# Gated recurrence: the first chunk, which holds the meta tokens, makes only its state

## What is computed

```python
h = concatenate([lead (112 zeros + 16 meta tokens), x])         # 1152 positions, nine chunks
log_f = where(valid, log(max(sigmoid(f_logit), TINY)), 0)       # decay
k     = where(valid, sigmoid(-f_logit), 0)                      # keys
# per chunk, with S the state carried in:
#   o_t = sum over s <= t of (q_t . decay(s..t) k_s) v_s  +  (q_t decay(start..t)) . S
#   S   = S * decay(whole chunk) + sum over s of decay(s..end) k_s v_s
o = rmsnorm(o, out_norm) * g
return h[:, CHUNK:]                                             # the first 128 positions are dropped
```

## Time and profile before

| | |
|---|---|
| median of the three runs shown | 3839.08 us (3838.89 to 3839.68) |
| the profiled execution's own time | 3837.87 us |
| its span, first to last instruction | 3836.2 us |
| mean granted TensorE clock | 0.976 of full speed |
| PE / PEld busy | 3654.7 us (95%) / 2955.8 us (77%) |
| DVE / ACT / POOL busy | 1888.6 us (49%) / 1240.2 us (32%) / 134.7 us (4%) |
| the stage `hg` in the span | about 2793 to 2913 us |

### The profile page before, as it was taken

The page is one execution under the profiler, slowest core; times in us unless marked ns, Lnnn a source line. Parts: engine busy times, 40 slices in busy tenths (PEclk is TensorE's granted clock), DMA queues, the critical chain, the costliest instruction groups (busy, mean ns, idle before and its releaser), DMA issues. The chain is left out here.

```text
span 3836.2 us, 49234 instructions
## 1 busy us (share of the span) xinstructions
PE 3654.7 (95%) x18404; PEld 2955.8 (77%) x18404; DVE 1888.6 (49%) x3690; ACT 1240.2 (32%) x2414; POOL 134.7 (4%) x143
## 2 busy tenths in 40 slices
PE   8999999989999999999999899998958999999999
PEld 6888888867777777777777787677947777787887
DVE  4244244363334455455555534544675657644343
ACT  3243133232323333332223434443322433233222
POOL 0000010000000000000000200000010000000000
PEclk9999999999999999999999999999978999999999
DMA  4222142221111121211111320111222322232223
GB/s 144 100 85 68 58 133 65 88 91 58 57 53 54 56 63 53 64 47 46 51 45 52 130 80 31 48 45 67 72 101 81 103 78 87 77 112 94 98 95 121
DMA packets 134598, 292.44 MB, mean 76 GB/s; under 512 B 31232, under 2 KB 70192, under 8 KB 134304
## 3 DMA queue, kind: packets, MB, share of 16 engines
q1 hardware_dynamic: 117552, 248.29, 19.4%
q0 software_dynamic: 14768, 33.49, 2.9%
q10 hardware_dynamic: 2112, 8.39, 0.6%
HBM read 244.49 MB, written 51.85 MB: 77 GB/s over the span
## 5 line engine op out<-in xcount | busy, mean ns | idle before, releaser
L142 DVE TENSOR_TENSOR all_w_lo<-all_w_raw,all_w_hi 128x1024 fp32r<-128x1024 f32 x311 | 380.6, 1224 | 289.5 <-ACT all_w_hi L137 288.8
L137 ACT ACTIVATE all_w_hi<-all_w_raw 128x1024 fp32r<-128x1024 f32 x311 | 326.7, 1051 | 504.9 <-PE om_z L152 261.5
L1076 PE MATMUL da_z<-all_hi,all_w_hi 128*128 128x512 f32 x736 | 305.9, 416 | 4.1 <-DVE all_w_lo L142 4.1
L1076 PE MATMUL da_z<-all_hi,all_w_lo 128*128 128x512 f32 x736 | 291.3, 396 | 0.0
L1076 PE MATMUL da_z<-all_lo,all_w_hi 128*128 128x512 f32 x736 | 289.7, 394 | 0.0
L152 PE MATMUL om_z<-all_hi,all_w_hi 128*128 128x512 f32 x640 | 257.3, 402 | 7.5 <-DVE all_w_lo L142 4.4
L945 ACT ACTIVATE da_pt<-da_tr 128x512 f32<-128x512 f32 (+1 forms) x192 | 101.0, 526 | 486.4 <-PE da_tr L1129 486.4
L152 PE MATMUL om_z<-all_hi,all_w_lo 128*128 128x512 f32 x640 | 255.6, 399 | 0.0
L953 ACT ACTIVATE at_p<-at_logit,da_pair_max 128x256 f32<-128x256 f32 (+1 forms) x384 | 177.9, 465 | 238.4 <-DVE da_pair_max L1332 238.1
L152 PE MATMUL om_z<-all_lo,all_w_hi 128*128 128x512 f32 x640 | 253.7, 396 | 0.0
L152 PE MATMUL pr_g<-all_hi,all_w_hi 128*128 128x344 f32 (+1 forms) x624 | 212.3, 340 | 10.1 <-issue 4.9
(11 more groups left out here) (569 smaller groups left out, 7568.4 us busy)
## 6 DMA issues: line engine op xcount, KB each, us to landing
all_w_raw<-in_w_mlp SPq DMA_DIRECT2D x128, 512.0 KB, 3.5
all_w_raw<-in_w_ug SPq DMA_DIRECT2D x48, 512.0 KB, 4.1
all_w_raw<-in_w_qkv SPq DMA_DIRECT2D x48, 512.0 KB, 3.7
all_w_raw<-in_w_in SPq DMA_DIRECT2D x27, 512.0 KB, 3.7
da_w_raw<-in_w_qkv SPq DMA_DIRECT2D x24, 512.0 KB, 3.5
all_w_raw<-in_w_bo SPq DMA_DIRECT2D x24, 512.0 KB, 3.5
all_w_raw<-in_w_v SPq DMA_DIRECT2D x20, 512.0 KB, 3.7
vhat<-ag_vst ACTq DMA_DIRECT2D x4, 2048.0 KB, 7.3
```

The source lines that it names most:

```text
L137: self.nc.scalar.activation(self.hi[b][:, :], self.raw[b][:, :], ACT.Copy).then_inc(self.hi_done[b], 1)
L142: self.nc.vector.tensor_tensor(self.lo[b][:, :], self.raw[b][:, :], self.hi[b][:, :].bitcast(F32), ALU.subtract).then_inc(self.lo_done[b], 1)
L1076: last = nc.tensor.matmul(z[h][:, :], wp[u][:, ws], ap[:, kk, cols], start=(kk == 0 and m == 0), stop=(kk == KT - 1 and m == 2))
```

## The change

For chunk 0, everything that only serves its outputs is left out: the load of its queries and gates, the levels of distances and their exponential, `dq` and `dk`, the scores, the masks, `qe`, the product with the state, the products with the values, the transposes of the gates, norm and gate. What stays of it: the load of forget logits and values, `sums`, `key`, `ecum`, `kend`, the four transposes, the copy `tm`, the product L2452 and `new_state`. The counts on semaphores of the left-out work go down by one chunk, so a wait that was for chunk c - 1 is written for the same chunk with another number. One wait is new: SP's load of chunk 2, which had waited for the scores, gates and `dq` of chunk 0, now waits for chunk 0's transposes (`s_tr`), right behind the request for `x`. The diff, cut to its core (line breaks of the code are kept, left-out parts show as "..."):

```diff
-        begins = lambda n: isinstance(n, int) and n == 0
+        lead = lambda c: c == 0
...
             def turn(n, b):
                 if n == 2:
                     sp.dma_start(x[:, :, :], x_in).then_inc(s_x, 16)
+                    sp.wait_ge(s_tr, 1)
                 if not ends(n):
 
-                    wait(sp, s_sc, 2 * (n - 1))
-                    wait(sp, s_gt, n - 1)
-                    wait(sp, s_dq, n - 1)
+                    wait(sp, s_sc, 2 * (n - 2))
+                    wait(sp, s_gt, n - 2)
+                    wait(sp, s_dq, n - 2)
                     cols = bass.ds(n * P, P)
-                    sp.dma_start(raw[b][:, 0:4, :], proj[U_HQ:U_HQ + 4, :, cols].rearrange("u p t -> p u t")).then_inc(s_raw[b], 16)
+                    if not lead(n):
+                        sp.dma_start(raw[b][:, 0:4, :], proj[U_HQ:U_HQ + 4, :, cols].rearrange("u p t -> p u t")).then_inc(s_raw[b], 16)
                     sp.dma_start(raw[b][:, 4:8, :], proj[U_HF:U_HF + 4, :, cols].rearrange("u p t -> p u t")).then_inc(s_raw[b], 16)
-                if not (isinstance(n, int) and n < 3):
-
-                    sp.wait_ge(s_out, n - 1)
+                if n >= 3:
+                    sp.wait_ge(s_out, n - 2)
                     sp.dma_start(o_cat[bass.ds((n - 3) * P, P), 3 * 4 * HD:], o[:, :, :].rearrange("p h d -> p (h d)")).then_inc(s_left, 16)
             for n in range(count + 1):
...
-            sp.wait_ge(s_out, count)
+            sp.wait_ge(s_out, count - 1)
...
-                    act.wait_ge(s_raw[b], 16 * (n - b) + 32)
+                    act.wait_ge(s_raw[b], 16 * n + 16)
...
-                if not begins(n):
+                if n:
                     act.wait_ge(s_tr, n)
-                    wait(act, s_op, 2 * (n - 1))
+                    wait(act, s_sp, n - 1)
+                    wait(act, s_op, 2 * (n - 2))
                     nc.scalar.activation(tm[:, :, :], pT[:, :].rearrange("p (u t) -> p u t", u=4), ACT.Copy).then_inc(s_tm, 1)
...
-                    act.wait_ge(s_dist, n + 1)
+                if not ends(n) and not lead(n):
+                    act.wait_ge(s_dist, n)
                     nc.scalar.activation(dist[:, :, :, :], dist[:, :, :, :], ACT.Exp).then_inc(s_ed, 1)
-                if not begins(n):
-                    act.wait_ge(s_ss, n)
+                if n >= 2:
+                    act.wait_ge(s_ss, n - 1)
...
-                if ends(n):
+                if ends(n) or lead(n):
                     return
-                pool.wait_ge(s_ed, n + 1)
...
-                if begins(n):
-                    pool.wait_ge(s_kz, 1)
-                wait(pool, s_sc, 2 * (n - 1))
+                wait(pool, s_sc, 2 * (n - 2))
...
+                if n == 0:
                     return
                 c, b = n - 1, 1 - b
-                pe.wait_ge(s_dq, c + 1)
-                pe.wait_ge(s_dk, c + 1)
-                scores(c, b, 0)
+                if not lead(c):
+                    pe.wait_ge(s_dq, c)
+                    pe.wait_ge(s_dk, c)
+                    scores(c, b, 0)
 
                 pe.wait_ge(s_kend, c + 1)
                 wait(pe, s_tm, c)
...
-                wait(pe, s_o, c)
-                pe.wait_ge(s_qe, c + 1)
-                pe.wait_ge(s_state, c + 1)
-                for hp in range(2):
-                    last = nc.tensor.matmul(pO[hp][:, 0:P], qe[b][:, hp, :], state[:, hp, :], start=True, stop=False, skip_group_check=True)
...
-                wait(pe, s_out, c)
-                for u in range(2):
-                    last = nc.tensor.transpose(pG[:, u * P:u * P + P], raw[b][:, 2 + u, :], ident)
-                last.then_inc(s_gt, 1)
+                if not lead(c):
+                    wait(pe, s_o, c - 1)
+                    pe.wait_ge(s_qe, c)
+                    pe.wait_ge(s_state, c + 1)
+                    for hp in range(2):
+                        last = nc.tensor.matmul(pO[hp][:, 0:P], qe[b][:, hp, :], state[:, hp, :], start=True, stop=False, skip_group_check=True)
+                    last.then_inc(s_used, 1)
+                    scores(c, b, 1)
+                    wait(pe, s_out, c - 1)
+                    for u in range(2):
+                        last = nc.tensor.transpose(pG[:, u * P:u * P + P], raw[b][:, 2 + u, :], ident)
+                    last.then_inc(s_gt, 1)
                 pe.wait_ge(s_tm, c + 1)
                 for hp in range(2):
                     last = nc.tensor.matmul(pS[:, hp * P:hp * P + P], tm[:, hp, :], tm[:, 2 + hp, :], start=True, stop=True)
                 last.then_inc(s_sp, 1)
-                values(c, 0)
-                values(c, 1)
+                if not lead(c):
+                    values(c, 0)
+                    values(c, 1)
...
-                if begins(n):
+                if lead(n):
...
-                wait(dve, s_used, n - 1)
+                if lead(n):
+                    return
+                wait(dve, s_used, n - 2)
                 nc.vector.tensor_tensor(qe[b][:, :, :], ecum[b][:, :, :], raw[b][:, 0:2, :], ALU.mult).then_inc(s_qe, 1)
...
             def new_state(c, b):
-
-                chain_o.start(c, 2)
                 dve.wait_ge(s_sp, c + 1)
-                dve.wait_ge(s_used, c + 1)
+                wait(dve, s_used, c)
...
-                new, old, c = not ends(n), not begins(n), n - 1
...
-                if new:
+                if new and not lead(n):
                     distances(n)
...
-                if old:
+                if n:
                     new_state(c, 1 - b)
-                if new:
+                if new and not lead(n):
                     queries(n, b)
```

More of the change, by code:

```diff
@@ L2315, in schedule @@
         def schedule(eng, turn):
-            turn(0, 0)
-            turn(1, 1)
-            for n in range(2, count + 1):
+            for n in range(count + 1):
                 turn(n, n % 2)
-        begins = lambda n: isinstance(n, int) and n == 0
+        lead = lambda c: c == 0
         ends = lambda n: n == count
@@ L2405, in scores @@
             def scores(c, b, hp):
-                wait(pe, s_masked, 4 * c + 2 * hp)
+                wait(pe, s_masked, 4 * (c - 1) + 2 * hp)
                 for l in range(NL):
@@ L2416, in values @@
                 for h in range(2):
-                    pe.wait_ge(s_masked, 4 * c + 2 * hp + h + 1)
+                    pe.wait_ge(s_masked, 4 * (c - 1) + 2 * hp + h + 1)
                     for l in range(NL):
@@ L2437, in turn @@
                 last.then_inc(s_tr, 1)
-                wait(pe, s_o, c)
-                pe.wait_ge(s_qe, c + 1)
-                pe.wait_ge(s_state, c + 1)
-                for hp in range(2):
-                    last = nc.tensor.matmul(pO[hp][:, 0:P], qe[b][:, hp, :], state[:, hp, :], start=True, stop=False, skip_group_check=True)
-                last.then_inc(s_used, 1)
-                scores(c, b, 1)
-                wait(pe, s_out, c)
-                for u in range(2):
-                    last = nc.tensor.transpose(pG[:, u * P:u * P + P], raw[b][:, 2 + u, :], ident)
-                last.then_inc(s_gt, 1)
+                if not lead(c):
[10 more added lines that the diff above has]
+                    last.then_inc(s_gt, 1)
                 pe.wait_ge(s_tm, c + 1)
@@ L2470, in sums @@
                 dve.wait_ge(s_soft, n + 1)
-                wait(dve, s_sc, 2 * (n - 1))
+                wait(dve, s_sc, 2 * (n - 2))
                 wait(dve, s_end, n)
@@ L2485, in distances @@
                 dve.wait_ge(s_cum, n + 1)
-                wait(dve, s_dk, n)
+                wait(dve, s_dk, n - 1)
                 flat = cum[:, :, :].rearrange("p h t -> p (h t)")
@@ L2505, in ends_of_keys @@
                 nc.vector.tensor_tensor(kend[b][:, :, :], kend[b][:, :, :], key[b][:, :, :], ALU.mult).then_inc(s_kend, 1)
-                wait(dve, s_used, n - 1)
+                if lead(n):
+                    return
+                wait(dve, s_used, n - 2)
                 nc.vector.tensor_tensor(qe[b][:, :, :], ecum[b][:, :, :], raw[b][:, 0:2, :], ALU.mult).then_inc(s_qe, 1)
             def queries(n, b):
-                dve.wait_ge(s_ed, n + 1)
+                dve.wait_ge(s_ed, n)
                 nc.vector.tensor_tensor(wide(dq[b]), wide(dist), over(raw[b][:, 0:2, :]), ALU.mult).then_inc(s_dq, 1)
             def mask(c, hp):
-                dve.wait_ge(s_sc, 2 * c + hp + 1)
-                wait(dve, s_op, 2 * c - 1 + hp)
+                dve.wait_ge(s_sc, 2 * (c - 1) + hp + 1)
+                wait(dve, s_op, 2 * (c - 1) - 1 + hp)
                 for h in range(2):
@@ L2531, in squares @@
             def squares(c):
-                dve.wait_ge(s_op, 2 * c + 2)
+                dve.wait_ge(s_op, 2 * c)
                 wait(dve, s_left, 16 * (c - 1))
@@ L2541, in output @@
             def output(c):
-                dve.wait_ge(s_rr, c + 1)
+                dve.wait_ge(s_rr, c)
```

(8 more changed lines are left out.)

7 lines of the change are left out of this document (3 added, 4 removed).

## The result

| | before | after |
|---|---|---|
| median of seven runs each | 3838.89 us (3832.80 to 3843.26) | 3821.53 us (3817.99 to 3827.06) |
| the profiled execution's own time | 3837.87 us | 3820.23 us |
| its span | 3836.2 us | 3818.7 us |
| the stage, from SP's first issue to its last store | 117.10 us | 99.48 us |
| from that store to the end of the span | 926.06 us | 926.66 us |

The ratio is 0.9956, with a 95% interval from 0.9946 to 0.9965: 17.4 us less. The forecast was a gain of 16.0 us and a time of 3823.1 us, with a range of 3819.5 to 3827.5, in which the measured time lies. The stage alone gives 117.10 - 99.48 = 17.62 us in the profiled executions. It starts 0.48 us earlier, and the work behind it takes 0.6 us more (926.66 against 926.06 us), which is no more than further traces scatter (927.14 us for the kernel before, 927.37 twice for the kernel after).

The account below looks back on a forecast made before the run. DVE was taken to bound each 19.42 us turn of the gated recurrence stage, with POOL's dk also on the path. 19.4 - 4.5 + 1.1 = 16.0 us saved, giving 3823.1 us, range 3819.5 to 3827.5.

Parts of the forecast that it names:

- Term one, a turn less: Gated recurrence stage: four chunks instead of five pass through scores to norm and gate, saving one steady period, 19.42 us.
- Term two, the lead-in: Before the first scores: chunk 1 starts behind chunk 0's last exponential, so dq and dk start 4.5 us later; bounds 4.1, 9.
- Term three, the first load: Stage start: without the load ahead, the forget logits land earlier and ACT starts 1.1 us sooner; bounds 0.5 and 1.6.
- The clock: TensorE's level at the stage's tail and next stage, kept unchanged in the sum; rivals worse 3827.2 us, better 3820.0, each 0.10.
- the rival's 1.5: Clock-better rival: last scores at the fast level save 1.5 us, next stage 1.6; total saving 19.1 us; chance 0.10.
- The rule that was weighed: Slow TensorE clock unless active: points against a stage losing a fifth of its products; taken as a rival, costing 4.1 us.
- The gain nearly gone: Rival: lead-in takes its 9 us bound and the clock is worse too; saving 7.4 us, time 3831.7; chance 0.04.
- The late load: Rival: chunk 2's load lands behind x; free until 2816.6, then one us per us, possibly making it slower; chance 0.02.

Follow-up runs that it names:

- experiment 4: Kernel before with 28 of chunk 0's 32 products with values on PE left out; stage 119.08 us, against 118.82 and 117.10 in two traces before.
- experiment 2: Kernel after with chunk 0's unused load of queries and gates put back; first ACT step 6.29 us into the stage against 5.44, stage 102.48 against 102.11.
- experiment 3: Kernel after with chunk 2's load made to wait for POOL's dk of chunk 1; stage 105.57 us, 3.5 more than the second trace after.

## Why the prediction was right

**Term one, a turn less.** Right to 0.01 us between the two first traces. The method, costing by the period and not by the removed work, is what experiment 4 bears out: 28 products of chunk 0 were worth nothing. The reason given beside it was too strong, though. "TensorE's clock is not what sets a turn" held for the turns of the first trace and not in general: where PE is slow from the second scores until the values begin, PE sets a turn at 19.85 to 20.25 us. It also follows that a turn less is worth up to 0.8 us more in an execution that has such a turn at that place.

**Term two, the lead-in.** Forecast 4.5, measured 4.13, near the lower bound of 4.1 and the same in all three traces of the kernel after. The mechanism was right at each point: ACT's order sets chunk 1's start, `tm` and PE's work fit in, POOL's `dk` and DVE exclude each other as before. The size was off by two small steps. Chunk 1's first ACT step comes 4.61 us after chunk 0's and not 4.74, since an ACT instruction starts before the one ahead has ended in the trace. And from there to the exponential there are 2808.26 - 2802.08 = 6.18 us, where chunk 0's 6.66 less 0.28 for the memset give 6.38: without the memset of L2478 the scans start 0.36 us sooner behind the instruction ahead of them, and DVE starts 0.12 us sooner behind ACT.

**Term three, the first load.** Forecast 1.1, measured 0.87, 0.85 in experiment 2, and 1.05 between the means of all traces. In the first traces the issue slot gave 0.48 us of it, as reckoned, and the way to landing the rest: the load took 4.4 us and not 4.8, nor the 4.2 of the row that was taken for it.

**The clock.** It was left as it was in the sum, and both ways were named as rivals. That the stage gained 1.6 us more than forecast in the first traces is luck: they fell on the better side at the tail (1.56 us, the rival's 1.5), and two later traces of the same kernel did not. The next stage did not start better. Its first large product came 17.57 us behind the last store, against 16.66 before, and 18.04 (before), 18.31 and 18.72 (after) in the further traces. The first large products were slow in all of them, four to six in number, where the prediction had about eight. The rule that was weighed, that the slow clock is the default and activity releases it (the Trainium skill's "TensorE: Matmul & The Clock Gate", "What's actually happening"), did not turn against the change by a size that these runs can tell. The mean granted clock of the stage alone was 0.81 and 0.79 before, and 0.79, 0.77 and 0.77 after: that is the way the rule points, by no more than one kernel scatters. Over the whole span it stayed (0.976 before, 0.978 after), since the stage is about a fortieth of it. The terms without the clock give 19.42 - 4.13 + 0.87 = 16.2 us, and the two timed comparisons, 17.4 and 15.9 us, lie on either side of it.

**The rivals.** The gain nearly gone needed a lead-in of 9 us; it was 4.13. The late load has the limit and the price that were worked out (experiment 3), with 6.5 us to spare for ACT's step. It was reckoned to land by 2814.6 at the worst and landed at 2810.1, 1.5 us behind `x` (2794.51 + 14.1 = 2808.6), as loads taken in order would.

## What to carry to other kernels

Where a stage is a pipeline of equal turns, a unit of work taken out is worth the period less what its remainder adds to the lead-in, whatever the sum of the removed instructions; find the period at one instruction of the bounding engine, and walk the lead-in in the order of the engine that is first in line. Before you call an engine's clock harmless, look at a turn in which it was slow at its worst place, or at a second trace: equal turns at unequal clocks showed a reserve, not how large it was. And before removing work from the bounding engine, ask how far the second one is behind: here it was 2.0 us in a turn of 19.4 with PE fast, and nothing with PE slow at the wrong place.

## What the hardware showed that was not expected

- The same kernel shows turns of 19.4 and of 20.25 us in one execution. The long ones need both slow second scores (3.35 us instead of 1.83) and slow steps behind them; with 3.36 us for the scores alone, a turn still took 19.43. The stage scatters by 2.6 us over three traces of the kernel after: 0.8 from such a turn, 1.6 from the tail, and 0.6 from the first load (4.82 to 5.44 us into the stage).
- A mask of 128x1024 elements that reads PSUM ran beside POOL's instruction in 2.35 us, while instructions with both inputs in SBUF stood for up to 4.18 us, 0.42 by themselves.
- Ten small products right ahead (2.39 us, then 1.43 us idle) did not bring TensorE to its fast level for the scores behind them (3.36 us, in both kernels that had them).
